# Loading the gate and up weights of each expert in four parts of 1 MB instead of eight of 512 KB

## What is computed

```python
def grouped_moe(t, w_router, b_router, w_gu, w_dn):      # t: (tokens, 1024)
    ...
    for e in range(N_EXPERTS):                            # 16
        g_, u_ = jnp.split(t @ w_gu[e], 2, axis=-1)       # w_gu[e]: 1024 x 1024
        out = out + gates[:, e:e + 1] * ((jax.nn.silu(g_) * u_) @ w_dn[e])   # w_dn[e]: 512 x 1024
```

## Time and profile before

| | |
|---|---|
| time, median of 3 runs | 2003.49 us (1999.81 to 2008.18) |
| time of the profiled execution | 2015.61 us |
| its span | 2013.8 us |
| PE busy | 1714.7 us (85%) |
| VectorE, ScalarE, GpSimd busy | 641.6 us (32%), 331.9 us (16%), 129.3 us (6%) |
| mean DMA rate | 181 GB/s over the span |
| gate and up loads | x256 of 512 KB, 7.5 us from issue to landing |
| down loads | x128 of 512 KB, 6.7 us from issue to landing |
| expert stage of layer 0, of layer 1 | about 820 to 1190 us, about 1690 to 1975 us |

### The profile page before, as it was taken

The page is one execution under the profiler, slowest core; times in us unless marked ns, Lnnn a source line. Parts: engine busy times, 40 slices in busy tenths (PEclk is TensorE's granted clock), DMA queues, the critical chain, the costliest instruction groups (busy, mean ns, idle before and its releaser), DMA issues.

```text
span 2013.8 us, 29796 instructions
## 1 busy us (share of the span) xinstructions
PE 1714.7 (85%) x12508; PEld 1001.9 (50%) x12508; DVE 641.6 (32%) x1538; ACT 331.9 (16%) x730; POOL 129.3 (6%) x149
## 2 busy tenths in 40 slices
PE   5999999999999996789877755999989976777852
PEld 2454566554444585344433324767778863333311
DVE  3089336671110136101100005764641133000003
ACT  1001135521000102111110101014520020110100
POOL 0200000000000001111111110000000001111100
PEclk9999999999999997999989976999999987899976
DMA  9524545602123324674489984332015534889894
GB/s 308 139 84 140 195 157 184 192 23 87 54 72 94 104 76 184 247 299 159 158 312 350 365 281 133 108 104 74 1 52 160 171 133 163 342 326 361 340 365 152
DMA packets 188823, 365.06 MB, mean 181 GB/s; under 512 B 23285, under 2 KB 107773, under 8 KB 187923
## 3 DMA queue, kind: packets, MB, share of 16 engines
q1 hardware_dynamic: 176784, 331.48, 46.9%
q0 software_dynamic: 10704, 25.16, 3.6%
q10 hardware_dynamic: 1203, 6.51, 0.9%
HBM read 356.79 MB, written 14.42 MB: 184 GB/s over the span
## 4 chain that ended last, share of the span: by engine, by line
PE 67%; DMA 20%; DVE 7%; SPq 3%; ACT 2%; issue 1%; another core or an unknown queue 0%; DVEq 0%; POOLq 0%; ACTq 0%
PE psum L782 64%; DMA ring<-in_moe_w_gu 14%; DMA ring<-in_moe_w_dn 3%; SPq L669 2%; SPq L645 1%; PE psum L966 1%; PE psum L1176 1%; DMA arena<-ys 1%; DMA ring<-in_w_mod 1%; DVE arena L1802 1%; PE psum L1199 0%; PE psum L844 0%; ACT uT L1290 0%; DVE H L2058 0%; DMA ys<-qkT,y_row 0%
## 5 line engine op out<-in xcount | busy, mean ns | idle before, releaser
L782 PE MATMUL psum<-uT,ring 128*128 128x512 f32 (+1 forms) x1472 | 505.2, 503 | 3.3 <-ACT uT L1290 3.3
L782 PE MATMUL psum<-ring,mo_tok 128*32 128x256 f32 x4992 | 351.9, 408 | 110.3 <-DMA ring<-in_moe_w_gu 104.4
L782 PEld LDWEIGHTS psum<-uT,ring 128*128 128x128 f32 x1472 | 281.1, 192 | 222.8 <-issue 204.1
L782 PEld LDWEIGHTS psum<-ring,mo_tok 128*32 128x32 f32 x4992 | 145.7, 114 | 267.3 <-DMA ring<-in_moe_w_gu 167.7
L782 PE MATMUL psum<-ring,v_tok 128*32 128x256 f32 x2496 | 177.2, 419 | 33.3 <-DMA ring<-in_moe_w_dn 26.9
L2032 DVE TENSOR_TENSOR qkT<-psum,qkT 128x128 f32<-128x128 f32 x78 | 22.8, 292 | 404.8 <-ACT qkT L1493 280.1
L782 PEld LDWEIGHTS psum<-ring,v_tok 128*32 128x32 f32 x2496 | 81.3, 121 | 119.2 <-DMA ring<-in_moe_w_dn 46.9
L1672 DVE SCALAR_TENSOR_TENSOR convT<-upad,cwT,convT 128x512 f32<-128x512 f32 (+1 forms) x240 | 132.4, 614 | 2.1
L736 POOL DMA_INDIRECT ys<-qkT,y_row x78 | 77.4, 992 | 592.3 <-ACT qkT L1500 572.0
L782 PE MATMUL psum<-ring,uT 128*128 128x256 f32 (+1 forms) x576 | 113.7, 357 | 0.0
L1500 ACT ACTIVATE qkT<-psum,mqk 128x256 f32<-128x256 f32 x78 | 37.0, 474 | 457.6 <-PE psum L782 457.6
(11 more groups left out here) (284 smaller groups left out, 1428.2 us busy)
## 6 DMA issues: line engine op xcount, KB each, us to landing
ring<-in_moe_w_gu SPq DMA_DIRECT2D x256, 512.0 KB, 7.5
ring<-in_moe_w_dn SPq DMA_DIRECT2D x128, 512.0 KB, 6.7
ring<-in_w_in SPq DMA_DIRECT2D x104, 512.0 KB, 4.7
ring<-in_w_mod SPq DMA_DIRECT2D x96, 512.0 KB, 6.2
ring<-in_w_out SPq DMA_DIRECT2D x16, 512.0 KB, 4.5
ring<-in_w_a_out SPq DMA_DIRECT2D x8, 512.0 KB, 3.5
ring<-in_w_b_out SPq DMA_DIRECT2D x8, 512.0 KB, 4.5
ring<-in_w_c_out SPq DMA_DIRECT2D x16, 256.0 KB, 3.0
```

The source lines that it names most:

```text
L782: return nc.tensor.matmul(dst, lhsT, rhs, start=start, stop=stop)
```

## The change

The gate and up weights come in four loads of 1 MB. Pair i is parts 2i and 2i + 1, which are one ring slot; each partition gets two neighbouring rows of w_gu[e], one run of 8 KB. A pair has one landing semaphore (`w_loaded` shrinks from 12 to 8), and SP waits for the use of the pair's second part before it issues the pair. PE waits for the pair wherever it waited for one of its parts. `w_used` and the order of PE's work stay as they are, as do the four down loads.

```diff
-        w_loaded = [sem(f"expert_part_loaded{x}") for x in range(NX)]
+        w_loaded = [sem(f"expert_part_loaded{x}") for x in range(KD // 2 + FT)]
         w_used = [sem(f"expert_part_used{x}") for x in range(NX)]
...
             def load_expert(l):
-                gu = a["moe_w_gu"][l].rearrange("e (p k) n -> k e p n", k=KD)
+                gu = a["moe_w_gu"][l].rearrange("e (p x k) n -> x e p (k n)", x=KD // 2, k=2)
                 dn = a["moe_w_dn"][l].rearrange("e (x p) n -> x e p n", x=FT)
-                parts = [gu[x] for x in range(KD)] + [dn[x] for x in range(FT)]
+                parts = [(2 * x, 2, gu[x]) for x in range(KD // 2)] + [(KD + x, 1, dn[x]) for x in range(FT)]
...
-                    for x in range(NX):
+                    for i, (x, width, src) in enumerate(parts):
                         n = index[("expert", l, x // 2)]
                         if e:
-                            sp.wait_ge(w_used[x], before_e + blk_base[l])
+                            sp.wait_ge(w_used[x + width - 1], before_e + blk_base[l])
                         elif x % 2 == 0:
                             sp.wait_ge(stream[n - NS][1], stream[n - NS][2])
-                        sp.dma_start(ring[:, n % NS, (x % 2) * D:(x % 2 + 1) * D], parts[x][e])\
-                            .then_inc(w_loaded[x], 16)
+                        sp.dma_start(ring[:, n % NS, (x % 2) * D:(x % 2 + width) * D], src[e]).then_inc(w_loaded[i], 16)
...
-            for x in range(NX):
+            for x in range(KD // 2 + FT):
                 sp.wait_ge(w_loaded[x], 16 * NE * DEPTH)
...
                     for k in pieces:
-                        pe.wait_ge(w_loaded[k], loads)
+                        pe.wait_ge(w_loaded[k // 2], loads)
...
                     for x in range(FT):
-                        pe.wait_ge(w_loaded[KD + x], loads)
+                        pe.wait_ge(w_loaded[KD // 2 + x], loads)
```

## The result

The changed kernel took 2050.53 us (median of 4 runs, 2049.03 to 2054.13), the kernel before 2005.71 us (4 runs, 1999.81 to 2008.18): a ratio of 1.023, 95% interval 1.020 to 1.026, or 45 us slower. Its profiled execution took 2049.65 us with a span of 2047.9 us. That is 34 us over the profiled span of before, which was itself longer than each of the four executions behind the median. Every ratio in this document leaves out executions more than 1.5% above the shortest of their kernel, which most of the kernels have now and then.

What follows compares the result with a forecast made beforehand. The prediction took the release of part 8, which holds back each expert's first down load, as the tight loop. Its terms, 38 - 2 + 4 - 12 = +28 on 2003.5, gave about 2032 us, range 2010 to 2052.

Steps and rivals of the forecast that it cites:

- The high corner: Upper end of the forecast range: 38 + 8 + 4 - 0, given as +50, near 2052 us.
- The down release: Expert changes: part 4 lands with part 5, so down loads are released 1.27 us later, 30 times; +38, less 2.
- the clock: PE's longer rests may keep it at 1.2 GHz longer, slowing parts 4 and 8; 0 taken, +4 as bound.
- That nothing absorbs it: Both expert layers pay the later down release, since PE already waits for down parts; absorbed rival 1996 us, chance 0.12.
- The first pair: SP's wait for part 1 behind experts of three or more blocks, nine places; +4 us, bounds 0 and 8.
- Pair (4,5) on SP: SP issues the pair only with part 5; one microsecond of cover is left, so 0.
- Longer packets: Gate and up loads: 8 KB packets save each engine 0.4 us an expert, 30 times; -12 us, bounds 0 and -24.
- 1.1 us from issue to new data: At an expert's first down load, time taken from SP's issue until new data flow, read from DMA shares.
- The 1.7 us of lag: Parts 5 to 7 behind part 4: a landing is seen some 1.7 us after the engines moved the data.
- runs are cut at 4 KB: Rival on gate and up loads: slower as forecast but no packet gain; +40, 2044 us, chance 0.13.
- Fewer loads, less rest: Rival in expert stages: rest comes from turn-round at each load; -21 and -12 for packets, 1970 us, chance 0.07.

Runs made afterwards that it cites:

- the run with the one wait: Kernel before, all loads unchanged, in which PE at part 4 waits for part 5 as well; ratio 1.0258 to the kernel before.

## Why the prediction was right

It was right in the way and, at 2032 for 2050.5 us with a range of 2010 to 2052, barely in the size: 28 us forecast, 45 measured in its own group and 49 in the next, which on 2003.5 would have been just outside. (The high corner, 38 + 8 + 4, is +50 and 2053.5, not 2052.) That the range held is partly luck; the way and the mechanism are not. Step by step:

- **The down release** (+36 with what I took off) is the cause. It is shown from three sides: one wait in the old kernel gives 52 us, splitting pair (4,5) takes four fifths of the loss away, and moving the down product makes both kernels faster, by 50 and by 28 us. In the changed kernel's two traces the rest at the down issues grew by 36 and 39 us, as forecast. As a price it was too low: 42 us (37 to 48) where PE waits for all pairs, which is nearest to the change, and 52 (45 to 59) where it waits at part 4 alone. I moved part 4 by 1.27 us, the spacing of landings with nothing between; in the run with the one wait it was 1.46 over all experts. And the clock, for which I had taken 0 with +4 as a bound, lengthens the chain that everything waits for by 0.37 us an expert in that run, 11 us, and by 0.22 and 0.14 us in the two traces of the changed kernel, 4 to 7 us. I had the row for it (a granted clock of 0.50 in two windows) and priced it too low.
- **That nothing absorbs it** was right in both layers: their stages grew by 16 and 19 us.
- **The first pair** (+4) measured 5 us, with an interval that includes no cost at all.
- **Pair (4,5) on SP** (0) measured 9 us. The one microsecond of cover is seen in the trace and the cost is there all the same; this step failed, and its cause is open.
- **Longer packets** (-12) measured -14 in the run that changes them alone, -9 by the medians of the packets, and 3 us in the engine time of the two kernels.
- **Two readings.** I took 1.1 us from issue to new data; in the changed kernel's trace the first packet starts 0.96 us after the issue where the engines had run dry. And in the trace of before the engines had not moved part 7's last byte by 1719.1: its last packets end at 1720.35 and its last landing event is at 1720.77. The 1.7 us of lag run from where most engines have stopped, not from the last byte. Neither changes the sum.
- The sum of the measured parts, in the order release, SP, packets: 42 + 14 - 14 = 42, or 52 with the run of the one wait in the place of the first. Measured: 45 and 49. By the first sum the miss lies for 6 us in the release and for 10 in SP's waits, with a few us left over; by the second it is all in the release. The intervals don't decide between them.
- **What I said would be seen**: rest of about 2.5 us at the down issues (1.9 to 3.0 in the windows, 2.2 on average), a stage of layer 1 some 14 us longer (19), issues about 1 us further apart (1.3), 8 KB packets at under twice 172 ns (328 on average in layer 1). PE does wait at even parts only, but for 1.4 to 1.6 us in the rows above and not 2.5: the pairs land 2.49 us apart, and PE's own products fill the rest.
- **The rivals.** That runs are cut at 4 KB is out: SP's queue has 17280 packets for the same bytes as 25920 before, and 7680 of them are of 8 KB. Fewer loads, less rest, is out: the rest sits at the release, goes away when the order is changed, and stays when the loads are longer. So the Trainium skill's rule of at least 1 MiB per DMA (DMA: Bandwidth & Descriptors, Rules for kernel authors) isn't borne out for loads that queue: 512 KB loads kept the engines full at 404 to 411 GB/s, and the fastest kernel here has them; 1 MB loads reached 421 in such a window, 2 to 4% more, and the kernel with them is slower. The 2 us of fixed cost that the prediction gives beside the rule are what the Trainium skill's DMA: Bandwidth & Descriptors (Anatomy of one DMA) gives for DMAs issued by GpSimd; these loads are SP's.

## What to carry to other kernels

Where loads refill a ring that the consumer frees, ask of each load what its landing lets the consumer do, and which later load that frees; a larger load lengthens this loop by the time of the bytes added to it, and that doesn't show in the rate of the transfers. Look for the windows in which the DMA engines rest and for the issue they end with: here that found an edit of four lines in PE's order which gave 28 us, while the larger loads cost 45. Price a wait on PE's path with the slow clock that follows it.

## What was unexpected of the hardware

- The chain from a landing to the next issue had sharp lengths, 1.13 and 1.99 us, by the clock level that PE was granted after its wait: the same eight instructions took 0.64 or 1.08 us. In the run with the one wait the longer wait thus cost about a quarter more than its own length (0.37 for 1.46 us).
- The SP queue's packets for 94.38 MB of layer 1 took 247 us an engine whether gate and up came in 4 KB or 8 KB packets; yet within 1 MB loads the 8 KB runs were 14 us faster than pairs of 4 KB runs that lie 16 KB apart.
